# A conditioning matrix summed by GpSimd inside the first MLP, and twelve units of its kind ahead of the expert loop instead of sixteen

## Chip, core and metric

One core of a Trainium2 chip runs one program. The time is microseconds on the device for one execution. TensorE multiplies, VectorE, ScalarE and GpSimd work on tiles, SyncE (SP) issues DMAs.

## What is computed

Two blocks over 256 tokens of width 1024. The first has a mixer, cross-attention and a mixture of 32 experts (each 12.6 MB of float32 weights). The second has two layers, attention and then an MLP each, and every one of the four sublayers is conditioned on a vector `c`:

```python
def ada_modulation(c, w, b):
    m = jax.nn.silu(c) @ w + b
    shift, scale, gate = jnp.split(m[:, None, :], 3, axis=-1)
    return shift, scale, 1.0 + gate

def second_block(...):
    for layer in range(DEPTH_2):
        shift, scale, gate = ada_modulation(c, ada_w[layer, 0], ada_b[layer, 0])
        h = x * (1.0 + scale) + shift
        y = mixer_ab(...) if layer % 2 == 0 else mixer_c(...)
        x = layer_norm(DN_ALPHA * x + gate * y, ...)
        shift, scale, gate = ada_modulation(c, ada_w[layer, 1], ada_b[layer, 1])
        h = x * (1.0 + scale) + shift
        y = squared_relu_mlp(h, mlp_w1[layer], mlp_w2[layer])
        x = layer_norm(DN_ALPHA * x + gate * y, ...)
```

Each `ada_w` is 1024 x 3072, so that four of them are 50 MB, read for one vector-matrix product each.

## The kernel before

The weights come through SBUF slots of 2 MB, called granules; SP issues their DMAs in the order in which TensorE uses them, and waits for `granules_used` (`used`) before it overwrites a slot. An `ada_w` is cut into six units of 512 columns, 24 in all. A unit is 1024 x 512, 2 MB, and TensorE multiplies it against `cs`, which holds silu(c) in one column of 32 (`ada`, L1353). After a group of units ScalarE copies the bank out and `ada_combine` (L1365) adds up the quadrants. Units 0 to 15 stand ahead of the expert loop, at places given by `ADA_AT`, and fill TensorE's time there. Units 16 to 21 follow in the attention of the first layer (`late_main` L1779, `late_combine` L1789), units 22 and 23 in the attention of the second (`late3`), where VectorE copies their banks (`late_copies`, L2571).

Ahead of the loop the other weights are used in halves of 1 MB: ScalarE rounds a half (`half_hi`), VectorE takes the rest (`half_lo`), and TensorE multiplies three times (L1274). In order: `w_k`, `w_v`, `w_in`, `w_out`, `w_q`, `w_o`. `project(MEMT)` uses `w_v`. The expert loop streams 192 granules of 2 MB.

An MLP is 16 granules, w1 and w2 by turns, four to a turn of `mlp_group`: w1 (L1274 with `XT_r`) fills two banks, ScalarE takes ReLU (L1045) and square (L1048), VectorE the low part (L2701, L2705, which raises `mlp_lo`), and w2 (L1274 with `arena_r`) adds into four banks. Every granule is first split, by ScalarE into `w_hi` (L554) and VectorE into `w_lo` (L565). ScalarE's order is fixed: behind the two ReLUs of w1 granule g it splits granules g+2 and g+3, so granules 8 and 9 behind granule 6's. SP's loop (L726) issues fill n when TensorE is done with granule n-4. `gate_rows` (L1706) stands before the last group; the layer norm that follows the MLP needs it. GpSimd has nothing to do in the MLP.

Of the kernel before, what the change touches and what calls it, by code (L numbers as in the profile page):

```python
# [22 lines left out]
ALU = mybir.AluOpType  # L23
# [4 lines left out]
P = 128  # L28
# [72 lines left out]
LATE = 16  # L101
ADA_AT = [("k", 2), ("v", 3), ("mix", 4), ("q", 1), ("scores", 3), ("router", 3)]
ADA_GROUPS = [(0, 2, 7, 6), (2, 5, 7, 6), (5, 9, 3, 2), (9, 13, 6, 7), (13, 16, 1, 4)]
# [3 lines left out]
def pre_stream():  # L107
# [4 lines left out]
    for name, n in ADA_AT:  # L112
# [15 lines left out]
SIDE = {PRE.index(("ada", u)): SLOTS + i for i, u in enumerate((8, 9, 12, 13))}  # L128
SIDE_FILL = {8: 32, 9: 48, 12: 80, 13: 96}
# [5 lines left out]
HEAD = [("w_k", 0), ("w_k", 1), ("ada", 0), ("w_v", 0), ("ada", 1), ("w_v", 1), ("ada", 2), ("ada", 4), ("w_in", 0), ("ada", 3)]  # L135
TAIL = [("w_o", 0), ("w_o", 1), ("ada", 12), ("ada", 14), ("ada", 15), ("ada", 13)]
# [3 lines left out]
AHEAD = {("ada", 12): (0,), ("ada", 15): (1,), ("ada", 13): (2, 3, 4, 5)}  # L140
# [5 lines left out]
        + [("c_in", i) for i in range(6)] + [("late", 3)] + [("c_out", i) for i in range(2)] + [("mlp1", i) for i in range(16)])  # L146
R2 = 4
# [90 lines left out]
def build_program(nc, A, tab_d, dft_d, out_d):  # L238
    ctx = ExitStack()
    with ctx:  # L240
# [195 lines left out]
        def unit_parts(u):  # L436

            if u == 12:
                places = [XNf, arn(6144, 2048)]
            elif u in SIDE_FILL:  # L440
                places = [{8: slot(SLOTS - 1), 9: arn(2048, SLOT), 13: arn(0, SLOT)}[u]]
            else:
                places = [slot(slot_of(PRE.index(("ada", u))))]
# [70 lines left out]
        def half_hi(act, name, *hs):  # L514

            for h in hs:
                n = half_no(name, h)
                g, raw = half_raw(name, h)
                if n == 1:
                    act.wait_ge(sem("gain_landed"), 16)  # L520
                else:
                    act.wait_ge(landed[slot_of(g)], FILL[g])
# [61 lines left out]
        def _(sp):  # L584
# [3 lines left out]
            sp.dma_start(first[:, 0:2, :], src[:, 0:2, :]).then_inc(sem("gain_landed"), 16)  # L588
# [4 lines left out]
            def fill(g, name, i):  # L593
# [44 lines left out]
            for g in FILL_ORDER[2:]:  # L638
# [17 lines left out]
                if (name, i) == ("w_v", 1):  # L656
# [3 lines left out]
                                 A["norm_ffn"][0].rearrange("(j p k) -> p j k", p=P, k=2)).then_inc(sem("gain_landed"), 16)  # L660
# [41 lines left out]
            for name, i in POST:  # L702
                if name[:3] != "mlp":
                    if (name, i) not in POST[0:2]:
                        post_fill(name, i)
                    if (name, i) == ("ab_in", 2):
                        sp.wait_ge(sem("bias_lo"), 2)
                        sp.dma_start(nfin, A["norm_final"][None, :].to_broadcast((P, D))).then_inc(sem("nfin_landed"), 16)
# [7 lines left out]
                with sp.Fori(0, 4) as i:  # L716
                    for j in range(R2):
                        s = slot_of(g + j)
                        sp.wait_ge(used, i * R2 + (g + j - R2 + 1))
                        if j % 2 == 0:  # L720
                            src = w1[:, :, bass.ds(i * (2 * HW) + (j // 2) * HW, HW)]
                            dst = slot(s).rearrange("p (k n) -> p k n", k=8)
                        else:
                            src = w2[:, bass.ds(i * 8 + (j // 2) * 4, 4), :]
                            dst = slot(s).rearrange("p (k n) -> p k n", k=4)
                        sp.dma_start(dst, src).then_inc(landed[s], 16)  # L726
# [11 lines left out]
        def _(pool):  # L738
# [2145 lines left out]
```

## Time and profile before

| | |
|---|---|
| median of three runs | 1813.48 us (1813.35 to 1814.29) |
| the profiled execution, its own time | 1816.24 us |
| its span | 1814.3 us |
| TensorE busy | 96% |
| GpSimd busy | 1% |
| DMA, mean | 324 GB/s, 587.43 MB |
| TensorE's granted clock | 0.992 of full speed |

The span is what the rows below divide; the execution's own time has what lies around it. PE is TensorE, DVE VectorE, ACT ScalarE, POOL GpSimd, SP SyncE. A row of the timeline names the line of the kernel, the tiles written and read, shape and count, and in brackets the engine's idle time before it with what ended it. A float32 multiplication shows as two records.

### The profile page before, as it was taken

To read this page: it belongs to the slowest core of one execution; us is meant where nothing else is said; L and a number is where in the kernel's file an instruction comes from. 1 tells how busy PE (TensorE), PEld (TensorE's weight loads), DVE (VectorE), ACT (ScalarE), POOL (GpSimd) and SP (SyncE) were. 2 spreads that over 40 slices of the span, in tenths; PEclk is the share of its full clock that TensorE was granted. 3 is DMA by queue.
4 is the path that set the end of the run, shared out by engine and by line. 5 is a ranking of instruction groups with operands and counts; after the bars stand their busy time and mean duration, and the time that the engine had idled before them with its cause. 6 is when DMAs were issued, how large, how long until landed. Compare 5 with 4: busy or idle time off the path is not lost.

```text
span 1814.3 us, 24405 instructions
## 1 busy us (share of the span) xinstructions
PE 1743.7 (96%) x9906; PEld 1092.5 (60%) x9906; DVE 749.0 (41%) x1287; ACT 526.5 (29%) x698; POOL 26.6 (1%) x36
## 2 busy tenths in 40 slices
PE   8999999999999999999999999999899999999997
PEld 7688754444434434343434344375699888679986
DVE  4454342212212112121212121379865469676555
ACT  5344421111111111111111010248444453744442
POOL 0002000000000000000000000000000000000001
PEclk9999999999999999999999999998999999999999
DMA  9958899999999999999999999974355556435550
GB/s 350 348 212 336 316 404 426 428 427 428 428 428 428 428 428 428 429 429 428 428 429 428 429 429 429 418 282 177 116 186 185 192 194 228 153 116 185 185 208 24
DMA packets 96608, 587.43 MB, mean 324 GB/s; under 512 B 7150, under 2 KB 7364, under 8 KB 70948
## 3 DMA queue, kind: packets, MB, share of 16 engines
q1 hardware_dynamic: 95072, 582.27, 79.3%
q10 hardware_dynamic: 1476, 4.30, 0.7%
q8 instruction: 44, 0.72, 0.2%
q14 instruction: 16, 0.13, 0.0%
HBM read 585.51 MB, written 1.05 MB: 323 GB/s over the span
## 4 chain that ended last, share of the span: by engine, by line
PE 72%; DMA 20%; DVE 5%; ACT 2%; issue 1%; SPq 0%; DVEq 0%; ACTq 0%
PE bank L1274 31%; DMA ring<-in_w_gate_up 19%; PE bank L1587 15%; PE bank L1606 9%; PE bank L1533 4%; PE bank L1861 3%; PE bank L1353 1%; PE bank L1617 1%; PE bank L1265 1%; PE bank L1579 1%; DVE w_lo L565 1%; ACT arena L965 1%; DMA ring<-in_ada_w 1%; PE bank L1599 1%; PE bank L1988 0%
## 5 line engine op out<-in xcount | busy, mean ns | idle before, releaser
L1587 PE MATMUL bank<-ring,arena 128*64 128x512 f32 x2048 | 462.4, 597 | 28.4 <-DMA ring<-in_w_gate_up 27.8
L1587 PEld LDWEIGHTS bank<-ring,arena 128*64 128x64 f32 x2048 | 137.7, 136 | 319.3 <-issue 255.9
L1606 PE MATMUL bank<-ring,arena 128*64 128x512 f32 x1024 | 226.8, 595 | 3.3
L1274 PE MATMUL bank<-w_hi,arena_r 128*128 128x512 f32 x672 | 217.1, 391 | 1.9 <-DVE arena_r L2705 1.9
L565 DVE TENSOR_TENSOR w_lo<-ring,w_hi 128x4096 fp32r<-128x4096 f32 (+2 forms) x44 | 192.5, 4375 | 44.1 <-ACT w_hi L554 41.8
L2400 DVE TENSOR_SCALAR arena<-bank 128x512 f32<-128x512 f32 x32 | 22.1, 691 | 367.2 <-PE bank L1587 367.2
L963 ACT ACTIVATE arena<-arena,sb_tab 128x512 f32<-128x512 f32 x32 | 23.1, 722 | 508.7 <-DVE arena L2400 508.7
L554 ACT ACTIVATE w_hi<-ring 128x4096 fp32r<-128x4096 f32 (+2 forms) x43 | 152.3, 3583 | 31.6 <-DMA ring<-in_c_w_out 18.3
L1606 PEld LDWEIGHTS bank<-ring,arena 128*64 128x64 f32 x1024 | 71.9, 137 | 137.6 <-issue 132.1
L1274 PE MATMUL bank<-XT_r,w_hi 128*128 128x256 f32 x512 | 145.8, 285 | 4.4 <-DVE arena_r L2689 4.4
L1274 PE MATMUL bank<-arena_r,w_hi 128*128 128x256 f32 x512 | 144.9, 283 | 0.0
L1274 PE MATMUL bank<-XT_r,w_lo 128*128 128x256 f32 x512 | 144.9, 283 | 0.0
L1274 PEld LDWEIGHTS bank<-w_hi,arena_r 128*128 128x128 f32 x672 | 126.2, 188 | 29.3 <-DVE arena_r L2705 2.8
L1533 PEld LDWEIGHTS bank<-arena,sb_XN 128*128 128x128 f32 x1056 | 123.2, 192 | 26.9 <-issue 26.9
L1533 PE MATMUL bank<-arena,sb_XN 128*128 128x64 f32 x1056 | 128.4, 275 | 0.0
L1274 PE MATMUL bank<-w_lo,arena_r 128*128 128x512 f32 x304 | 118.6, 390 | 0.0
L2421 DVE SCALAR_TENSOR_TENSOR arena_r<-bank,sb_att,arena_r 128x512 fp32r<-128x512 f32 x32 | 24.0, 751 | 217.3 <-ACT arena_r L968 217.3
L1274 PEld LDWEIGHTS bank<-XT_r,w_hi 128*128 128x128 f32 x512 | 98.2, 192 | 5.8 <-issue 5.3
L1274 PEld LDWEIGHTS bank<-arena_r,w_hi 128*128 128x128 f32 x512 | 98.2, 192 | 0.9 <-issue 0.5
L1274 PEld LDWEIGHTS bank<-XT_r,w_lo 128*128 128x128 f32 x512 | 98.3, 192 | 0.0
L968 ACT ACTIVATE arena_r<-bank,sb_att 128x512 fp32r<-128x512 f32 x32 | 22.0, 687 | 231.0 <-PE bank L1606 231.0
L538 DVE TENSOR_TENSOR half_lo<-ring,half_hi 128x2048 fp32r<-128x2048 f32 x26 | 59.5, 2290 | 64.0 <-ACT half_hi L528 64.0
(415 smaller groups left out, 2104.6 us busy)
## 6 DMA issues: line engine op xcount, KB each, us to landing
ring<-in_w_gate_up SPq DMA_DIRECT2D x128, 2048.0 KB, 32.0
ring<-in_w_down SPq DMA_DIRECT2D x64, 2048.0 KB, 35.3
ring<-in_mlp_w SPq DMA_DIRECT2D x32, 2048.0 KB, 8.3
ring<-in_ada_w SPq DMA_DIRECT2D x21, 2048.0 KB, 13.1
ring<-in_c_w_in SPq DMA_DIRECT2D x6, 2048.0 KB, 7.7
ring<-in_w_in SPq DMA_DIRECT2D x4, 2048.0 KB, 8.8
ring<-in_w_v SPq DMA_DIRECT2D x2, 2048.0 KB, 9.6
ring<-in_w_out SPq DMA_DIRECT2D x2, 2048.0 KB, 11.9
```

Source lines behind the costliest of these rows:

```text
L538: eng.tensor_tensor(lo[:], half_raw(name, h)[1], hi[:].bitcast(F32), ALU.subtract).then_inc(sem("w_lo"), 1)
L554: ins = eng.activation(dst, raw, ACT.Copy) if on_act else eng.tensor_copy(dst, raw)
L565: eng.tensor_tensor(lo[:, 0:w], slot(slot_of(granule_no(name, i)), w), hi[:, 0:w].bitcast(F32), ALU.subtract).then_inc(sem("w_lo"), 1)
L963: act.activation(sig, gcl, ACT.Sigmoid, bias=zero, scale=1.702).then_inc(sem("e_sig"), 1)
L968: act.activation(y_hi, B[2][:], ACT.Copy, scale=slot_gate).then_inc(sem("e_y"), 1)
L1274: mm = pe.matmul(out, st[a], mv[b], start=start and a + b == 0, stop=stop and a == 1, skip_group_check=True)
L1533: mm = pe.matmul(B[3][:, k * CAP:(k + 1) * CAP], XN[:, t, k * P:(k + 1) * P], sel_tok[:, t, :], start=(t == 0), stop=(t == 1))
L1587: mm = pe.matmul(B[m][CAP * h:CAP * h + CAP, :], xe[:, 2 * j + kl, :], w[:, kl, m * D + h * HW:m * D + (h + 1) * HW], start=False, stop=(j ...
L1606: mm = pe.matmul(B[2][CAP * h:CAP * h + CAP, :], hT[:, c, CAP * j:CAP * j + CAP], w[:, c, h * HW:(h + 1) * HW], start=(j == 0 and c == 0), ...
L1861: mm = pe.matmul(b, x[:, k, t * P:(t + 1) * P], parts[wa][:, kl, width * c:width * c + width], start=k + xa + wa == 0, stop=False, skip_gr ...
L2400: dve.tensor_scalar(gcl, B[0][:], 7.0, None, ALU.min).then_inc(sem("e_clamp"), 1)
L2421: dve.scalar_tensor_tensor(y_lo, B[2][:], slot_gate, y_hi.bitcast(F32), ALU.mult, ALU.subtract).then_inc(sem("e_ylo"), 1)
```

## The change

`LATE` goes from 16 to 12: units 0 to 11 stand ahead of the loop, units 12 to 17 take the places that 16 to 21 had, and the last six, the whole matrix of the second MLP, go to the first MLP. There a unit comes in eight pieces of 128 x 512 (256 KB) through three places in the arena (`unit_raw`). GpSimd multiplies a piece by the column of silu(c) that belongs to it and adds it to the unit's sum (`unit_acc`, two places by turns); the first piece of a unit is a product alone, written to the sum. TensorE then sums over partitions by four multiplications with a column of ones (`unit_sums`), and one ScalarE copy reads all 24 columns. `late3`, its copies and combinations are gone. The SP and TensorE loops of the first MLP are written out, and its `gate_rows` stands behind the last w1 granule.

```diff
-LATE = 16
-ADA_AT = [("k", 2), ("v", 3), ("mix", 4), ("q", 1), ("scores", 3), ("router", 3)]
+LATE = 12
+ADA_AT = [("k", 0), ("v", 2), ("mix", 3), ("q", 1), ("scores", 3), ("router", 3)]
...
+        unit_raw = [arn(a, HW) for a in (4096, 4608, 7312)]
+
+        def unit_acc(n):
+
+            return XN[:, 1, HW * (n % 2):HW * (n % 2) + HW]
...
+                def unit_fill(m):
+
+                    w = A["ada_w_2"][1, 1].rearrange("(k p) n -> p k n", p=P)
+                    n = m // 8
+                    if m >= 3:
+                        sp.wait_ge(sem("unit_used"), 2 * (m - 2))
+                    else:
+                        sp.wait_ge(*upto("mlp0", "mlp_lo", 1))
+                    sp.dma_start(unit_raw[m % 3], w[:, m % 8, HW * n:HW * n + HW]).then_inc(
+                        sem(f"unit{m % 3}_landed"), 16)
+
+                if l == 0:
+                    for n in range(16):
+                        if n >= R2:
+                            for m in range(4):
+                                unit_fill(4 * (n - R2) + m)
+                        mlp_fill(n // 4, n % 4)
...
+            pool.wait_ge(*upto("mlp0", "mlp_lo", 1))
+            for m in range(48):
+                n, kl = m // 8, m % 8
+                pool.wait_ge(sem(f"unit{m % 3}_landed"), 16 * (m // 3 + 1))
+                raw, acc, by = unit_raw[m % 3], unit_acc(n), sil[:, 1, kl:kl + 1]
+                if kl == 0:
+                    if n >= 2:
+                        pool.wait_ge(sem("late_comb"), 6 + n - 1)
+                    pool.tensor_scalar(acc, raw, by, None, ALU.mult).then_inc(sem("unit_used"), 2)
+                else:
+                    pool.tensor_scalar(raw, raw, by, None, ALU.mult).then_inc(sem("unit_used"), 1)
+                    pool.wait_ge(sem("unit_used"), 2 * m + 1)
+                    pool.tensor_tensor(acc, acc, raw, ALU.add).then_inc(sem("unit_used"), 1)
...
+                    if l == 0 and last and p == 0:
+                        act.wait_ge(sem("late_comb"), 12)
+                        act.activation(mod[:, 3, :], B[6][:, 0:24], ACT.Copy).then_inc(sem("late_read"), 1)
+                    elif l == 0 and last:
+                        gate_rows(1)
...
-            project(MEMT, 0, between={2: first_units, 4: ada_combine, 6: mix_turn})
+            project(MEMT, 0, between={6: mix_turn})
             chunk_ready("mix", KC - 1)
-            ada(3)
+            pe.wait_ge(sem("cs"), 2)
+            ada(2)
...
-            ada(4)
+            ada(3)
...
+                    if l == 0 and p == 1:
+                        if last:
+                            pe.wait_ge(sem("late_read"), 3)
+                            gate_rows(1)
+                        elif it:
+                            unit_sums(it - 1)
...
+                    if l == 0 and last:
+                        unit_sums(2)
+
+            def unit_sums(i):
+
+                for n in (2 * i, 2 * i + 1):
+                    pe.wait_ge(sem("unit_used"), 16 * n + 16)
+                    for c in range(4):
+                        mm = pe.matmul(B[6][:, 4 * n + c:4 * n + c + 1], unit_acc(n)[:, c * P:(c + 1) * P], ones[:, 0:1],
+                                       start=True, stop=True)
+                    mm.then_inc(sem("late_comb"), 1)
```

SP's queue from the last fills before the first MLP on, before (the loop of four fills, whose ISA rows hold the wait) and then now:

```order
L684 DMA ring<-in_ab_w_out 128x4x1024 [waits granules_used] x2
L716 UNCONDITIONAL_BRANCH
L716 ISA
L726 ISA [waits granules_used]
L726 DMA ring<-in_mlp_w_2 128x8x512
L719 REGISTER_ALU
L726 ISA [waits granules_used]
L726 DMA ring<-in_mlp_w_2 128x4x1024
```

```order
L689 DMA ring<-in_ab_w_out 128x4x1024 [waits granules_used] x2
L732 DMA ring<-in_mlp_w_2 128x8x512 [waits granules_used]
L732 DMA ring<-in_mlp_w_2 128x4x1024 [waits granules_used]
L732 DMA ring<-in_mlp_w_2 128x8x512 [waits granules_used]
L732 DMA ring<-in_mlp_w_2 128x4x1024 [waits granules_used]
L742 DMA arena<-in_ada_w 128x512 [waits mlp_lo] x3
L742 DMA arena<-in_ada_w 128x512 [waits unit_used]
L732 DMA ring<-in_mlp_w_2 128x8x512 [waits granules_used]
L742 DMA arena<-in_ada_w 128x512 [waits unit_used] x4
L732 DMA ring<-in_mlp_w_2 128x4x1024 [waits granules_used]
```

Four pieces of `ada_w` now stand between two fills of `mlp_w`, in front of the later one; they wait for GpSimd (`unit_used`).

TensorE behind the w1 part of granule 6, before and then now (`w_hi_49` and `w_lo_50` are granule 7, w2):

```order
L1274 MATMUL bank<-arena_r,w_hi_55 128x256
L1274 MATMUL bank<-XT_r,w_lo_56 128x256
L1915 REGISTER_ALU
L1930 REGISTER_ALU [waits w_lo]
L1274 MATMUL bank<-w_hi_49,arena_r 128x512 [waits mlp_lo]
L1274 MATMUL bank<-w_lo_50,arena_r 128x512
```

```order
L1322 MATMUL bank<-arena_r,w_hi_55 128x256
L1322 MATMUL bank<-XT_r,w_lo_56 128x256
L1988 MATMUL bank<-sb_tab,sb_XN 128x1 [waits unit_used]
L1988 MATMUL bank<-sb_tab,sb_XN 128x1 x3
L1988 MATMUL bank<-sb_tab,sb_XN 128x1 [waits unit_used]
L1988 MATMUL bank<-sb_tab,sb_XN 128x1 x3
L1322 MATMUL bank<-w_hi_49,arena_r 128x512 [waits mlp_lo,w_lo]
L1322 MATMUL bank<-w_lo_50,arena_r 128x512
```

The sums of units 0 and 1 (L1988) have come in between the two granules. The same rows stand again behind granules 10 and 13.

GpSimd from the end of unit 1 to the first pieces of unit 2, which are all new:

```order
L828 TENSOR_SCALAR arena<-arena,sb_sil 128x512 [waits unit2_landed]
L830 TENSOR_TENSOR sb_XN<-sb_XN,arena 128x512 [waits unit_used]
L828 TENSOR_SCALAR arena<-arena,sb_sil 128x512 [waits unit0_landed]
L830 TENSOR_TENSOR sb_XN<-sb_XN,arena 128x512 [waits unit_used]
L826 TENSOR_SCALAR sb_XN<-arena,sb_sil 128x512 [waits late_comb,unit1_landed]
L828 TENSOR_SCALAR arena<-arena,sb_sil 128x512 [waits unit2_landed]
L830 TENSOR_TENSOR sb_XN<-sb_XN,arena 128x512 [waits unit_used]
```

The first product of unit 2 (L826) waits for `late_comb`, which TensorE's sums raise.

## Rows read from the trace of the kernel before

**Rows 1.** Page of the profile: its first line
```profile
span 1814.3 us, 24405 instructions
```

**Rows 2.** Busy time of each engine by stage (columns as in the first line)
```profile
core 0: us, PE busy (x) PEld busy (x) DVE busy (x) ACT busy (x) POOL busy (x), PEclk, DMA share, GB/s
76.00:78.90 2.90, 2.90 (x17) 0.49 (x9) 1.01 (x1) 0.00 (x0) 0.00 (x0) 0.60 0.97 395
272.00:590.00 318.00, 316.87 (x1669) 138.00 (x1670) 69.29 (x154) 38.74 (x47) 0.00 (x0) 1.00 1.01 428
...
1308.00:1492.00 184.00, 182.63 (x1165) 165.88 (x1166) 108.17 (x83) 83.43 (x57) 0.00 (x0) 1.00 0.50 177
```

**Rows 3.** Chain of waits, two waits for DMA: start us, us, what
```profile
60.55 12.97 DMA ring<-in_ada_w
593.19 33.56 DMA ring<-in_w_gate_up
```

**Rows 4.** TensorE in order, 46 to 140 us: start us, us, instruction
```profile
46.41 3.64 PE L1353 MATMUL bank<-ring,sb_cs 128*32 128x512 f32 x32
...
69.27 1.92 PE L1353 MATMUL bank<-ring,sb_cs 128*32 128x512 f32 x16
73.57 5.34 PE L1353 MATMUL bank<-ring,sb_cs 128*32 128x512 f32 x32 [2.38 <-DMA ring<-in_ada_w]
...
132.72 7.08 PE L1353 MATMUL bank<-ring,sb_cs 128*32 128x512 f32 x64
```

**Rows 5.** VectorE, two instructions of the head
```profile
44.95 2.29 DVE L538 TENSOR_TENSOR half_lo<-ring,half_hi 128x2048 fp32r<-128x2048 f32 x1 [5.36 <-ACT half_hi L528]
...
138.82 1.65 DVE L2289 SCALAR_TENSOR_TENSOR arena_r<-bank,sb_col,arena_r 128x256 fp32r<-128x256 f32 x4
```

**Rows 6.** First MLP around granule 8: DMA issue, ScalarE, VectorE, TensorE
```profile
1365.01 0.37 SPq L726 DMA_DIRECT2D ring<-in_mlp_w  x1
...
1388.65 7.13 ACT L554 ACTIVATE w_hi<-ring 128x4096 fp32r<-128x4096 f32 x2
...
1392.30 8.96 DVE L565 TENSOR_TENSOR w_lo<-ring,w_hi 128x4096 fp32r<-128x4096 f32 x2 [2.76 <-ACT w_hi L554]
...
1387.10 0.40 PE L1274 MATMUL bank<-w_hi,arena_r 128*128 128x512 f32 x1
...
1398.00 0.28 PE L1274 MATMUL bank<-XT_r,w_hi 128*128 128x256 f32 x1
...
1409.52 0.40 PE L1274 MATMUL bank<-w_hi,arena_r 128*128 128x512 f32 x1
```

**Rows 7.** DMAs by line: KB of one, median us from issue to landing
```profile
ring<-in_mlp_w SPq DMA_DIRECT2D x32, 2048.0 KB, 8.3
sb_X<-in_x SPq DMA_DIRECT2D x1, 1024.0 KB, 17.3
```

**Rows 8.** GpSimd's groups: count | busy us, mean ns of one
```profile
L538 POOL TENSOR_TENSOR half_lo<-ring,half_hi 128x2048 fp32r<-128x2048 f32 x2 | 9.2, 4614 | 91.6 <-ACT half_hi L528 91.6
L773 POOL CAST w_hi<-ring 128x1224 fp32r<-128x1224 f32 x3 | 3.5, 1206 | 910.0 <-DMA ring<-in_ab_w_in 910.0
```

**Rows 9.** End of the program: GpSimd beside VectorE
```profile
1800.11 0.69 DVE L2621 SCALAR_TENSOR_TENSOR sb_X<-sb_X,sb_XN 128x512 f32<-128x512 f32 x1
1803.97 2.36 POOL L790 TENSOR_TENSOR sb_X<-sb_X,arena 128x1024 f32<-128x1024 f32 x1 [214.15 <-ACT sb_X L1009]
1805.55 1.33 DVE L2621 SCALAR_TENSOR_TENSOR sb_X<-sb_X,sb_XN 128x512 f32<-128x512 f32 x1
```

**Rows 10.** Second attention: VectorE's four copies, TensorE's combination
```profile
1567.17 0.42 DVE L2571 COPY sb_vec<-bank 128x256 f32<-128x256 f32 x1
1567.84 0.74 DVE L2571 COPY sb_XN<-bank 128x256 f32<-128x256 f32 x2
...
1584.03 1.95 PE bank L1789 x16
```

**Rows 11.** First MLP, the second part of its last granule: TensorE
```profile
1481.00 0.50 PE L1274 MATMUL bank<-w_hi,arena_r 128*128 128x512 f32 x1 [0.95 <-DVE arena_r L2705]
```

More of the change, by code:

```diff
@@ L127 @@
 R1 = 8
-SIDE = {PRE.index(("ada", u)): SLOTS + i for i, u in enumerate((8, 9, 12, 13))}
-SIDE_FILL = {8: 32, 9: 48, 12: 80, 13: 96}
+SIDE = {PRE.index(("ada", u)): SLOTS + i for i, u in enumerate((4, 5, 8, 9))}
+SIDE_FILL = {4: 32, 5: 48, 8: 80, 9: 96}
 RING = [g for g in range(NPRE) if g not in SIDE]
@@ L134 @@
 E_BLOCK = 4
-HEAD = [("w_k", 0), ("w_k", 1), ("ada", 0), ("w_v", 0), ("ada", 1), ("w_v", 1), ("ada", 2), ("ada", 4), ("w_in", 0), ("ada", 3)]
-TAIL = [("w_o", 0), ("w_o", 1), ("ada", 12), ("ada", 14), ("ada", 15), ("ada", 13)]
+HEAD = [("w_k", 0), ("w_k", 1)]
+TAIL = [("w_o", 0), ("w_o", 1), ("ada", 8), ("ada", 10), ("ada", 11), ("ada", 9)]
 FILL_ORDER = ([PRE.index(p) for p in HEAD] + [g for g in range(NPRE) if PRE[g] not in HEAD + TAIL]
@@ L145 @@
         + [("ab_out", i) for i in range(2)] + [("mlp0", i) for i in range(16)]
-        + [("c_in", i) for i in range(6)] + [("late", 3)] + [("c_out", i) for i in range(2)] + [("mlp1", i) for i in range(16)])
+        + [("c_in", i) for i in range(6)] + [("c_out", i) for i in range(2)] + [("mlp1", i) for i in range(16)])
 R2 = 4
@@ L715, in _, with mlp_fill @@
                 w2 = A["mlp_w2_2"][l].rearrange("(k p) n -> p k n", p=P)
[L716 to L726, printed above, removed]
+                def mlp_fill(i, j):
+                    s = slot_of(g + j)
+                    sp.wait_ge(used, i * R2 + (g + j - R2 + 1))
+                    if j % 2 == 0:
+                        src = w1[:, :, bass.ds(i * (2 * HW) + (j // 2) * HW, HW)]
+                        dst = slot(s).rearrange("p (k n) -> p k n", k=8)
+                    else:
+                        src = w2[:, bass.ds(i * 8 + (j // 2) * 4, 4), :]
+                        dst = slot(s).rearrange("p (k n) -> p k n", k=4)
+                    sp.dma_start(dst, src).then_inc(landed[s], 16)
+                def unit_fill(m):
[13 more added lines that the diff above has]
+                        mlp_fill(n // 4, n % 4)
+                else:
+                    with sp.Fori(0, 4) as i:
+                        for j in range(R2):
+                            mlp_fill(i, j)
                 g += 16
@@ L774, in _, with with_norm @@
                     *((sem("w_hi"), 1) if kl == 2 else (sem("ab_in_hi"), 1)))
-            last = mod[:, 3, :]
+            m2, m3 = mod[:, 2, :], mod[:, 3, :]
+            def with_norm(m, l, n):
+                pool.wait_ge(sem("late_mod"), n)
+                pool.tensor_tensor(part[:, 2], m[:, 8:16], cols("ln_b_2", 3)[:, l], ALU.mult).then_inc(sem("late_mod"), 1)
+                pool.wait_ge(sem("late_mod"), n + 1)
+                pool.tensor_tensor(m[:, 0:8], m[:, 0:8], part[:, 2], ALU.add).then_inc(sem("late_mod"), 1)
+                pool.tensor_tensor(m[:, 8:16], m[:, 8:16], cols("ln_g_2", 3)[:, l], ALU.mult).then_inc(sem("late_mod"), 1)
@@ L785, in _ @@
+            pool.wait_ge(sem("late_read"), 3)
+            pool.tensor_tensor(m3, m3, ada_bT[:, 72:96], ALU.add).then_inc(sem("late_mod"), 1)
+            with_norm(m3, 2, 6)
             split_hi(pool, "c_out", 1, on_act=False)
-            pool.wait_ge(sem("late_read"), 3)
-            pool.tensor_tensor(last[:, 16:24], last[:, 16:24], ada_bT[:, 88:96], ALU.add).then_inc(sem("late_mod"), 1)
             pool.wait_ge(*upto("ln3", "ln_landed", 32))
@@ L951, in _ @@
             act.wait_ge(sem("bias_landed"), 16 * 8)
-            act.wait_ge(*done("ada", 13))
+            act.wait_ge(*done("ada", 9))
             for m in range(2):
@@ L1936, in mlp_group @@
                     mm.then_inc(used, 1)
-            def mlp(l):
-                with pe.Fori(0, 3) as it:
-                    mlp_group(l, it, False)
-                gate_rows(2 * l + 1)
-                mlp_group(l, 3, True)
+                    if l == 0 and last:
[7 more added lines that the diff above has]
+                    mm.then_inc(sem("late_comb"), 1)
+            def mlp(l):
+                if l == 0:
+                    for it in range(4):
+                        mlp_group(0, it, it == 3)
+                else:
+                    with pe.Fori(0, 3) as it:
+                        mlp_group(l, it, False)
+                    gate_rows(2 * l + 1)
+                    mlp_group(l, 3, True)
                 at[0] += 16
@@ L2561, in front @@
                                       ALU.subtract).then_inc(sem("nm"), 1)
-            def late_copies():
-                for u, b in ((LATE + 6, 6), (LATE + 7, 7)):
-                    if u == LATE + 6:
-                        dve.wait_ge(sem("late_mm"), 4)
-                    else:
-                        dve.wait_ge(*done("late", 3))
-                    for i, part in enumerate(late_part(u)):
-                        dve.tensor_copy(part, B[b][:, i * S:(i + 1) * S]).then_inc(sem("late_part"), 1)
             def attend(st, mask, ot, after_front):
```

107 lines of the change are left out of this document (41 added, 66 removed).

## Prediction

> **What bounds the kernel now.** The page first: TensorE is busy nearly throughout, so I read which wait ends last in each stage [rows 1, 2]. From 272 to 590 us the DMA engines carry 428 GB/s [rows 2], and from 593 us the chain of waits names `in_w_gate_up` once per two experts [rows 3]. A loop whose DMA never rests ends when the bytes have passed, so it moves by exactly as much as its start moves. Before the loop TensorE goes without gaps apart from a wait of 2.38 us for `in_ada_w` [rows 4]. In the first MLP TensorE is busy 182.63 of 184 us, with DMA at half load (177 GB/s) [rows 2]. There, what TensorE receives late, the program gets late.
>
> **The head: four units fewer.** One unit is 16 records of `ada`: 3.64 us for two units, 7.08 for four [rows 4], so 1.78 each.
> - Units 0 and 1 go from the middle of `project(MEMT)`: 3.6. But they covered VectorE: `half_lo` runs 44.95 to 47.24 [rows 5], and TensorE now wants that half at 46.41 [rows 4]. 0.8 comes back. Gain 2.8.
> - One combination (L1365, eight records) goes: half of the 1.95 of 16 such records [rows 10], less some overlap: 0.8.
> - `ada(3)` becomes `ada(2)`. Before, the first unit begins at 69.27; then comes a wait of 2.38 us for the second, which stood behind `w_in` in the queue (12.97 us) [rows 3]; and the two that follow take 5.34 where 46.41 shows 3.64 for the same [rows 4], since the granted clock fell to 0.60 behind the wait [rows 2], toward the 1.2 GHz level. The end is 78.91, 9.6 after the start. Now the units are asked for before all of `w_in`, so 3.6. Gain 6.0.
> - `ada(4)` becomes `ada(3)`: 1.8, but the output projection's second token tile waits for L2289, which ends at 140.47 [rows 5]; it would be wanted at 139.3. Gain 0.6.
>
> Sum 2.8 + 0.8 + 6.0 + 0.6 = **10.2 us**. All later issues into the ring follow TensorE or the splits behind it, so I let the experts' stream, and the loop's end, move by the same. Bounds: 8 if another cover is gone, 12 if nothing comes back. The work between loop and MLP has as many units as before: 0.
>
> **The first MLP, the queue.** Granules are numbered 0 to 15, even w1, odd w2; w1 takes 11.5 us on TensorE (1398.00 to 1409.52), w2 10.9 [rows 6]. SP asked for granule 8 at 1365.01, when granule 4 was done; ScalarE splits it from 1388.65, 3.57 us, VectorE from 1392.30, 4.48, and TensorE takes it at 1398.00 [rows 6]: slack 1.2 us behind ready data.
>
> Now four pieces stand before each fill from 4 on, and the fourth waits until the first of them is worked off. Piece 16 begins unit 2, whose sum goes where unit 0's is. It waits for `late_comb`, that is for TensorE's sums behind granule 6. So fill 8 can't be issued until granule 6 is done, the very time at which ScalarE wants it landed. The same holds for fill 12 and granule 10 (unit 4, piece 32). This is a mechanism of the written order and doesn't depend on how fast GpSimd is.
>
> Prices. A combination of two units, 16 records, is 1.95 us [rows 10]; a new sum is eight records: 0.9. A fill lands 8.3 us after its issue [rows 7], a piece (0.26 MB at 428 GB/s) adds 0.6. What is issued behind a large transfer lands behind it: `in_x` took 17.3 us for 1 MB [rows 7]. A GpSimd sum: 4614 ns for 2048 columns [rows 8], so 1.2 for 512. A product by one column a partition isn't in the trace: below, the cast of 1224 columns in 1206 ns, 0.5 [rows 8]; above, the sum's 1.2; I take 0.8, as it too reads one tile. A piece with its wait: 2.1.
>
> Step by step, in the time of before:
> - Granule 6 ends 1387.1, `late_comb` rises at 1388.2, product done 1389.3 (VectorE is at its own two), piece 19 and fill 8 issued by 1389.7, landed +8.9 = 1398.6. Split: +3.57 + 4.48 = 1406.7. Granule 8 starts 8.7 late, 1.8 of it the two sums.
> - Fill 9 waits for piece 20, landed behind fill 8 at 1399.2, done 1401.3; issued 1401.7, landed 1410.6, split 1418.7, and VectorE then still makes the hidden tile's low part (1.5: two instructions of 0.69, as one of that shape in [rows 9], and a wait): granule 9 at 1420.2, 10.7 late.
> - Fill 10 waits for a product alone: in time. Fill 11 issued 1424.4, landed 1433.3, in time but for sums (1.8): granule 11 at 1444.4, ended 1455.3.
> - `late_comb` 1443.7, fill 12 issued 1445.0, landed 1453.9, split 1462.0: granule 12 starts there, and granule 13 at 1475.5 by the steps of 9.
> - Granule 13 ends 1486.4, sums to 1488.2, granule 14 to 1499.7. Fill 15 is issued 1479.7, landed 1488.6; `c_in` 0 behind it 1493.5; ScalarE is at its split to 1497.1 before it takes up granule 14's ReLU, VectorE to 1501.6, then twice 1.5. The second part of granule 15 starts at 1504.5, not 1481.00 [rows 11]: **23.5 us later**.
>
> The moved gate rows cost the same in either place. Unrolled loops I cost at nothing: the head is straight code, and TensorE runs it without gaps.
>
> **What rides on it.** A two-input VectorE instruction took 1.33 us beside a GpSimd sum, 0.69 without it [rows 9]. On the path such pairs meet some two times: +1.3 (0 to 8). Behind its 2.38 us wait TensorE lost 5.34 - 3.64 = 1.7 us to the clock [rows 2, 4]; behind the two waits of 7 us I add that twice: +3.4 (0 to 8, for five waits).
>
> The Trainium skill (SBUF — State Buffer, "SBUF: two separate sides") says that a VectorE instruction with two SBUF inputs and a GpSimd instruction exclude one another for their whole length. The trace agrees: 1805.55 plus 1.33 ends 0.55 after GpSimd's sum does. What it would make of this MLP is the second rival.
>
> **The second attention.** VectorE's four copies (1567.17 to 1568.58) and TensorE's combination (1.95) stood on the chain [rows 10]. I take 1.2 of the first and 1.0 of the second, as the next weights are ready only then. Gain **2.2** (0 to 3.2).
>
> **Sum.** -10.2 + 23.5 + 1.3 + 3.4 - 2.2 = +15.8. The profiled span 1814.3 [rows 1] becomes 1830.1; its execution took 1816.24, 2.76 above the median of the three runs, so that I add the sum to the median: 1813.48 becomes **1829.3**.
>
> **Rivals.**
> - The forecast, 0.67: 1817 to 1837. Its lower end has both bounds of the last part at nothing, the head at 12 and a stall less.
> - The two engines' exclusion becomes a bound, 0.14. Per granule VectorE's two-input work is 4.48 [rows 6] and 1.4 us, GpSimd's four pieces 4 x (0.8 + 1.2) = 8.0, together 13.9 of the 11.2 that a granule takes. Behind each hard stall the fills then follow every 13.9 instead of 11.4 us, some 4 us more each: 1837.3. For it: [rows 9]; against it: TensorE's own stalls give the engines time. By the rule that the skill's page states, it would be this.
> - It comes out faster, 0.11: fill 8 isn't held. If piece 16 were done by 1380 (8.9 before ScalarE's 1388.65), the MLP would cost its six sums, 5.4, and the total be 1813.5 - 10.2 - 2.2 + 5.4 = 1806.5. Against it: the wait as written; for it, that I may have misread which sum frees unit 2's place.
> - More gain ahead of the loop, 0.05: 8.4 MB less at 428 GB/s are 19.6 us, if DMA and not TensorE set the experts' start: 1819.9. Against it: the fills there wait for TensorE's releases.
> - The loop takes the head's gain back, 0.03: 1839.5.
>
> A difference under 0.2% (3.6 us) is what a measurement here can't tell from none. Slower than 1817.1: 0.83; faster than 1809.9: 0.11; between: 0.06, from the lower edge of the forecast. Range 1815 to 1840: it holds the forecast and three rivals, and leaves out the faster case.
>
> **What would show it.** `w_in` starts near 69.3 on TensorE instead of 78.9, and the last expert ends 10 earlier. In the MLP TensorE waits some 7 us ahead of granules 8 and 12 for VectorE's `w_lo`, ScalarE waits for the DMA `in_mlp_w`, GpSimd waits long at the first product of units 2 and 4, and SP issues fill 8 only behind granule 6. Fills at their old distance would prove me wrong; so would a product far above 1.2 us, or a loop that ends where it did.

## The result, and the profile after

The changed kernel takes **1859.55 us** (median of six runs, 1856.74 to 1862.97) against 1813.55 us: ratio 1.0253, interval 1.0242 to 1.0264. Slower was forecast, but by 15.8 us; it is 46, outside the range. The profiled execution has a span of 1861.1 us, 46.8 above [rows 1].

Where the 46.8 are, from the chain of waits, here of the kernel before, then of the changed one (start, us, what):

```profile
1308.24 6.84 PE bank L1274 x55
1490.82 0.45 PE bank L1841 x4
1622.21 134.77 PE bank L1274 x864
```

```profile
68.46 3.06 PE bank L1322 x24
...
1299.67 33.87 PE bank L1322 x238
...
1538.20 0.45 PE bank L1878 x4
...
1667.32 136.18 PE bank L1322 x864
```

The first MLP begins 8.6 us earlier (1308.24 to 1299.67), lasts 238.5 instead of 182.6, **56.0 us more**; the second attention behind it is 2.3 shorter (131.4 to 129.1), and the same 864 records of the second MLP take 1.4 longer, as the clock of its first 53 us is 0.97. The forecast had 28.2 more for this MLP (23.5 + 1.3 + 3.4), so 27.8 of the 31 us that it missed are here. Busy time in it, before and after (columns as in [rows 2]):

```profile
1308.24:1490.82 182.58, 181.63 (x1158) 165.08 (x1159) 106.82 (x80) 82.55 (x55) 0.00 (x0) 1.00 0.50 178
```

```profile
1299.67:1538.20 238.53, 200.30 (x1206) 181.53 (x1207) 120.65 (x80) 83.65 (x56) 183.92 (x94) 0.91 0.53 190
```

TensorE is idle 38.2 us instead of 1.0, which gives 37.3 of the 56.0, and busy 18.7 longer. 4.8 of this are the six sums (0.8 each in the chain); the other 13.9 are the same records at a mean granted clock of 0.91 of full speed (2.4 GHz) instead of 1.00. What TensorE waits for (us in total, times, longest), and then GpSimd's groups:

```profile
PE bank L1322 <- DVE w_lo L570: 17.8, 3, 6.8
PE bank L1988 <- POOL sb_XN L830: 13.5, 1, 13.5
PE bank L1322 <- DVE arena_r L2746: 6.9, 4, 3.1
```

```profile
L828 POOL TENSOR_SCALAR arena<-arena,sb_sil 128x512 f32<-128x512 f32 x42 | 94.7, 2254 | 2.4 <-DMA arena<-in_ada_w 2.4
L830 POOL TENSOR_TENSOR sb_XN<-sb_XN,arena 128x512 f32<-128x512 f32 x42 | 64.9, 1545 | 3.5
L826 POOL TENSOR_SCALAR sb_XN<-arena,sb_sil 128x512 f32<-128x512 f32 x6 | 20.4, 3398 | 68.5 <-DMA arena<-in_ada_w 55.5 <-PE bank L1988 12.9
```

The three waits for `w_lo` end at 1403.9, 1435.8 and 1469.6: they are ahead of granules 8, 10 and 12. The first of them:

```profile
1403.92 0.39 PE L1322 MATMUL bank<-XT_r,w_hi 128*128 128x256 f32 x1 [4.86 <-DVE w_lo L570]
```

The prediction had 8 and 12. The wait of 13.5 us for the last sums, behind granule 13, it didn't have at all. GpSimd works without pause but for 12.9 us at the written hold and 2.4 for DMAs. The timeline around fill 10 shows why it has no time to spare (start, us, engine, line):

```profile
1396.49 1.57 POOL L828 TENSOR_SCALAR arena<-arena,sb_sil 128x512 f32<-128x512 f32 x1 [1.14 <-DMA arena<-in_ada_w]
1398.14 1.28 POOL L830 TENSOR_TENSOR sb_XN<-sb_XN,arena 128x512 f32<-128x512 f32 x1
1399.40 5.82 POOL L828 TENSOR_SCALAR arena<-arena,sb_sil 128x512 f32<-128x512 f32 x1
...
1412.40 6.25 POOL L826 TENSOR_SCALAR sb_XN<-arena,sb_sil 128x512 f32<-128x512 f32 x1
```

```profile
1399.44 4.43 DVE L570 TENSOR_TENSOR w_lo<-ring,w_hi 128x4096 fp32r<-128x4096 f32 x1 [11.60 <-ACT w_hi L559]
1411.38 5.33 DVE L570 TENSOR_TENSOR w_lo<-ring,w_hi 128x4096 fp32r<-128x4096 f32 x1 [7.51 <-ACT w_hi L559]
```

A product with nothing beside it is 1.56 to 1.57 us and a sum 1.28. The product that begins beside `w_lo` takes 5.82: 1.57 and nearly all of VectorE's 4.43. At 1411.38 it is the other way round first: `w_lo` takes 5.33, since a sum is still running, and then the product waits for it. SP's fills show what comes of it:

```profile
1313.68 0.43 SPq L732 DMA_DIRECT2D ring<-in_mlp_w  x1
...
1386.87 0.43 SPq L732 DMA_DIRECT2D ring<-in_mlp_w  x1
...
1399.82 0.43 SPq L732 DMA_DIRECT2D ring<-in_mlp_w  x1
...
1419.06 0.43 SPq L732 DMA_DIRECT2D ring<-in_mlp_w  x1
...
1497.11 0.43 SPq L732 DMA_DIRECT2D ring<-in_mlp_w  x1
```

Twelve fills, 4 to 15, from 1313.68 to 1497.11: one in 16.7 us, where TensorE uses a granule in 11.2. Four pieces of GpSimd's own time, 0.08 being the gap between product and sum, are 4 x (1.56 + 1.28 + 0.08) = 11.7; one `w_lo` that it can't run beside makes 16.1.

### The profile page after: what moved, and what is told of

It reads as the page before. It is cut to its first block, busy times and chain, and to the rows that moved or that the text cites. A ratio compares the mean times of both kernels' runs of the same rounds, so it can differ in the third digit from the quotient of the medians.

```text
span 1861.1 us, 24308 instructions
## 1 busy us (share of the span) xinstructions
PE 1747.9 (94%) x9834; PEld 1104.2 (59%) x9834; DVE 761.5 (41%) x1282; ACT 527.0 (28%) x697; POOL 210.0 (11%) x129
## 4 chain that ended last, share of the span: by engine, by line
PE 64%; DMA 22%; DVE 5%; POOL 4%; ACT 3%; issue 1%; SPq 0%; DVEq 0%; ACTq 0%; POOLq 0%
PE bank L1322 27%; DMA ring<-in_w_gate_up 20%; PE bank L1630 14%; PE bank L1649 8%; PE bank L1576 4%; PE bank L1898 2%; POOL arena L828 2%; PE bank L1660 1%; POOL sb_XN L830 1%; DMA arena<-in_ada_w 1%; DVE w_lo L570 1%; POOL sb_XN L826 1%; DMA ring<-in_mlp_w 1%; PE bank L1622 1%; PE bank L1313 1%
## 5 line engine op out<-in xcount | busy, mean ns | idle before, releaser
L570 DVE TENSOR_TENSOR w_lo<-ring,w_hi 128x4096 fp32r<-128x4096 f32 (+2 forms) x44 | 198.3, 4507 | 114.9 <-ACT w_hi L559 113.3
L1322 PE MATMUL bank<-XT_r,w_hi 128*128 128x256 f32 x512 | 150.6, 294 | 22.3 <-DVE w_lo L570 17.8
L1322 PE MATMUL bank<-arena_r,w_hi 128*128 128x256 f32 x512 | 149.2, 291 | 0.0
L1322 PE MATMUL bank<-XT_r,w_lo 128*128 128x256 f32 x512 | 149.2, 291 | 0.0
L1322 PEld LDWEIGHTS bank<-XT_r,w_hi 128*128 128x128 f32 x512 | 103.0, 201 | 24.6 <-DVE w_lo L570 19.1
L1322 PEld LDWEIGHTS bank<-arena_r,w_hi 128*128 128x128 f32 x512 | 102.9, 201 | 0.6 <-issue 0.2
L1322 PEld LDWEIGHTS bank<-XT_r,w_lo 128*128 128x128 f32 x512 | 102.6, 200 | 0.0
L828 POOL TENSOR_SCALAR arena<-arena,sb_sil 128x512 f32<-128x512 f32 x42 | 94.7, 2254 | 2.4 <-DMA arena<-in_ada_w 2.4
```

Of the source, the lines that this page charges most:

```text
L570: eng.tensor_tensor(lo[:, 0:w], slot(slot_of(granule_no(name, i)), w), hi[:, 0:w].bitcast(F32), ALU.subtract).then_inc(sem("w_lo"), 1)
L828: pool.tensor_scalar(raw, raw, by, None, ALU.mult).then_inc(sem("unit_used"), 1)
L1322: mm = pe.matmul(out, st[a], mv[b], start=start and a + b == 0, stop=stop and a == 1, skip_group_check=True)
```

## Experiments

The theories as the expectations name them: **A**, the forecast, is the written hold (piece 16 behind TensorE's sums after granule 6, piece 32 after granule 10). **B** is GpSimd's pace, its own time and VectorE's exclusive instructions; it is the forecast's second rival with a dearer product. **C** is the chain in SP's order (fill, piece landed behind it, work, next fill).

Times are medians; the kernel before took 1814.1 to 1814.7 beside them. The last column is the length of the first MLP in the profiled execution, from the start of ScalarE's first `XT_r` row ahead of it to that of the first behind it, which leaves out the head and the attention: it begins at 1305.5 before and somewhere between 1291.7 and 1298.0 in the kernels with the new head.

| kernel | us | ratio to before, interval | MLP |
|---|---|---|---|
| before | 1813.55 | | 185.8 |
| changed | 1859.55 | 1.0253 (1.0242, 1.0264) | 241.8 |
| 1 no pieces, sums stay | 1806.01 | 0.9958 (0.9944, 0.9972) | 189.9 |
| 2 small GpSimd work | 1824.23 | 1.0058 (1.0042, 1.0075) | 205.9 |
| 3 no hold | 1858.14 | 1.0240 (1.0223, 1.0257) | 239.8 |
| 4 no product | 1840.37 | 1.0145 (1.0128, 1.0162) | 221.7 |
| 5 small work, no hold | 1807.41 | 0.9960 (0.9947, 0.9972) | 190.0 |
| 6 GpSimd free | 1817.57 | 1.0018 (1.0007, 1.0028) | 192.3 |
| 7 GpSimd's own queue | 1890.12 | 1.0421 (1.0403, 1.0438) | 270.8 |
| 8 VectorE instead | 1808.20 | 0.9965 (0.9953, 0.9978) | 189.9 |
| 9 `w_lo` by a copy | 1837.55 | 1.0126 (1.0110, 1.0141) | 222.2 |
| 10 pieces behind the fill | 1862.94 | 1.0268 (1.0252, 1.0284) | 242.3 |
| 11 as 8, again | 1807.44 | 0.9961 (0.9948, 0.9975) | 190.0 |
| 12 copy, no hold | 1828.59 | 1.0076 (1.0059, 1.0093) | 211.2 |

**1. What is left without the pieces.**

```diff
-                        if n >= R2:
-                            for m in range(4):
-                                unit_fill(4 * (n - R2) + m)
...
-            for m in range(48):
-                n, kl = m // 8, m % 8
...
-                    pe.wait_ge(sem("unit_used"), 16 * n + 16)
```

> Leaves out the 48 pieces: their DMAs and GpSimd's products and sums; TensorE's 24 sums over partitions read what stands there, and stay where they are. It measures what is left of the change, the head, the second attention and the sums. From the profile of after the first MLP begins 8.6 us earlier than before, the second attention is 2.3 us shorter, the six sums are 6 x 0.8 = 4.8 us. Every theory: 1813.5 - 8.6 - 2.3 + 4.8 = 1807.4 us. A time well above it would say that the unrolled loops, the earlier start or the place of the gate rows cost something by themselves.

1806.0, 1.4 under the expected time, so no cost of the unrolled loops, of the place of the gate rows or of the earlier start is seen. The head and the attention gain, the sums cost 4.1 in the MLP, and all that makes the kernel slow is in the pieces: 1859.6 - 1806.0 = 53.6 us.

**2. Small work on GpSimd, everything else as it is.**

```diff
-                    pool.tensor_scalar(raw, raw, by, None, ALU.mult).then_inc(sem("unit_used"), 1)
+                    pool.tensor_scalar(raw[:, 0:8], raw[:, 0:8], by, None, ALU.mult).then_inc(sem("unit_used"), 1)
```

(and so the other two instructions)

> GpSimd's product and sum take 8 of the 512 columns of each piece (the rest of the sum is left out); all DMAs, waits and the order stay. Theory A (the forecast: the written hold, fill 8 behind granule 6 and fill 12 behind granule 10, is the main cost): both holds stay, some 7 us each and some clock: about 1825 us. Theory B (GpSimd sets the pace: four pieces of 1.56 + 1.28 us and a w_lo of 4.4 us that it can't run beside, 16 us a fill where TensorE needs 11.2): the pace is gone, what is left is the hold where it shows: 1808 to 1825. Theory C (the chain fill, piece behind it in the ring, work, next fill, 12.2 us a fill, is the cost): without GpSimd's time 10 us a fill, as under A.

1824.2, and TensorE's waits inside this MLP are the two that the prediction had, ahead of granules 8 and 12:

```profile
PE bank L1322 <- DVE w_lo L570: 12.2, 2, 6.6
```

The hold exists and costs what A says, but 35 us of the 53.6 went with GpSimd's time.

**3. No hold, all the work.**

```diff
-            return XN[:, 1, HW * (n % 2):HW * (n % 2) + HW]
+            if n < 2:
+                return XN[:, 1, HW * n:HW * n + HW]
+            return arn(5264 + HW * (n - 2), HW)
...
-                    if n >= 2:
-                        pool.wait_ge(sem("late_comb"), 6 + n - 1)
+                    if n == 2:
+                        pool.wait_ge(*upto("ln0", "ln_x", 2))
...
-            load_ln(1, upto("ln0", "ln_x", 2))
             mlp_group(0, 3, True, ("c_in", 0))
+            load_ln(1, (sem("late_comb"), 12))
```

> All the work stays; units 2 to 5 get sums of their own in the space of the layer norm's gains (whose load moves behind the last sum), so that no product waits for TensorE's sums. A: both holds gone, most of the 56 us that the MLP grew by goes, under 1835. B: GpSimd was busy or blocked for all but 12.9 (hold) and 2.4 (DMA) of its 196.6 us, so at most 12.9 come back: 1847 or more. C: as B.

1858.1: A fails as the explanation of the 46. GpSimd's busy time rose by most of what the hold had left idle. The rows are of the changed kernel and then of this one, from 1311 us to the end of GpSimd's work; POOL is the figure ahead of the clock:

```profile
1311.00:1510.00 199.00, 160.77 (x958) 144.89 (x956) 94.35 (x44) 68.56 (x40) 179.06 (x90) 0.91 0.58 206
```

```profile
1311.00:1512.00 201.00, 164.84 (x974) 148.06 (x973) 98.02 (x43) 67.22 (x40) 188.62 (x90) 0.90 0.56 196
```

179.1 against 188.6 for the same 90 instructions: the 12.9 us of idle time had hidden 9.5 us of `w_lo`, beside which it would have stood blocked, and waits for DMAs grew by 2.2. From first product to last sum it is 197.9 and 196.7. TensorE's waits stand elsewhere: 6.2 us for the last sums, 29.9 for the low part of the hidden tile (`arena_r`, the squared activations that w2 multiplies). ScalarE, in its fixed order, splits the next granules first, and waits up to 18.5 us for the DMA of one before it takes up the ReLU from which that tile is made.

**4. Without the product of 42 pieces, about half of GpSimd's work.**

```diff
-                    pool.tensor_scalar(raw, raw, by, None, ALU.mult).then_inc(sem("unit_used"), 1)
-                    pool.wait_ge(sem("unit_used"), 2 * m + 1)
-                    pool.tensor_tensor(acc, acc, raw, ALU.add).then_inc(sem("unit_used"), 1)
+                    pool.wait_ge(sem("unit_used"), 2 * m)
+                    pool.tensor_tensor(acc, acc, raw, ALU.add).then_inc(sem("unit_used"), 2)
```

> Leaves out the product of 42 pieces: GpSimd adds the raw piece to the sum; the first piece of each unit keeps its product, all waits stay. A: the hold stays, GpSimd's part in it is small: above 1845. B: GpSimd needs 4 x 1.35 + 4.4 = 9.8 us a fill, under TensorE's 11.2: the pace falls away and only the hold is left: about 1825. C: the chain is 12.2 - 1.6 = 10.6 us: also about 1825.

1840.4 fits neither: it is 15 above B's 1825 (and C's), and 5 below A's bound. 19 us went with the product, so GpSimd's time counts, but B's 9.8 us a fill, with `w_lo` in it, should have left the hold alone. TensorE still waits twice at the hold (14.0 us for `w_lo`, where kernel 2 has 12.2), and besides 5.1 for the hidden tile and 1.7 for the last sums. The sums now meet `w_lo` instead of the products, as their mean shows:

```profile
L829 POOL TENSOR_TENSOR sb_XN<-sb_XN,arena 128x512 f32<-128x512 f32 x42 | 92.2, 2195 | 25.2 <-DMA arena<-in_ada_w 18.9 <-POOL sb_XN L829 5.2 <-POOL sb_XN L826 1.0
```

2195 ns instead of 1280: 38 us of blocked time stay with half of the work. The blocking isn't a share of GpSimd's time; it comes about once for each `w_lo`. Why this kernel is 16 us above kernel 2 isn't worked out beyond these waits and the clock (0.93 against 0.97 from 1300 to 1510 us).

**5. Small work and no hold**, the edits of 2 and 3 together.

> Eight of 512 columns for GpSimd's instructions, as in the run before (the rest of each sum is left out), and no product waits for TensorE's sums. What stays is the order in SP's queue: four pieces ahead of each fill through three places. If the hold accounts for all of the 18 us between 1824.2 (small work, hold kept) and 1806.0 (sums alone): 1806 to 1809. If the chain fill, piece behind it, next fill is a cost of its own (theory C): 1812 or more.

1807.4, within noise of 1. So the hold is worth 16.8 us here (1824.2 - 1807.4), and the order in SP's queue, with three places, nothing by itself: C is no cost of its own.

**6. GpSimd works, and neither SP nor TensorE waits for it.**

```diff
-                raw, acc, by = unit_raw[m % 3], unit_acc(n), sil[:, 1, kl:kl + 1]
+                raw, acc, by = unit_raw[m % 2], unit_raw[2], sil[:, 1, kl:kl + 1]
```

(no DMAs for pieces, as in 1; in the second attention ScalarE waits for the end of GpSimd's work before it copies into the arena)

> GpSimd does 48 products and 42 sums of 512 columns without any DMA, on three tiles that stay where they are, and neither SP nor TensorE waits for it (the sums over partitions read what stands there; the sums of the last six units are left out). It measures what GpSimd's work costs by sitting beside VectorE alone. Theory B in its strong form (VectorE is slowed as much as GpSimd): each granule's w_lo starts up to 1.6 us late with 1.2 us of slack: 1810 to 1816. If only GpSimd pays: 1806 to 1808, with products of about 6 us in the trace wherever a w_lo runs.

1817.6, 11.6 above 1 and above both expected ranges. In the MLP it costs 2.4 us (192.3 to 189.9), with both engines paying:

```profile
L827 POOL TENSOR_SCALAR arena<-arena,sb_sil 128x512 f32<-128x512 f32 x42 | 107.5, 2560 | 4.1
L829 POOL TENSOR_TENSOR arena<-arena 128x512 f32<-128x512 f32 x42 | 87.5, 2083 | 3.5
```

```profile
L570 DVE TENSOR_TENSOR w_lo<-ring,w_hi 128x4096 fp32r<-128x4096 f32 x15 | 72.9, 4861 | 16.3 <-ACT w_hi L559 15.4
```

VectorE's `w_lo` is 4.86 us instead of 4.43. Another 6.8 arise because GpSimd isn't done with the MLP: it works until 1522.9, and the second attention, which it now overlaps, takes 131.5 us from `XT_r` to `XT_r` where kernel 1 has 124.7. ScalarE's added wait isn't the cause: when it comes to that copy, after 1537, GpSimd has long been done, and it waits for TensorE. From first product to last sum GpSimd needs 214.4 us: 48 pieces beside VectorE at its normal pace take more time than this MLP has, even when nothing holds them up.

**7. The pieces in GpSimd's own queue**, with the edit of 3.

```diff
+            def own_fill(m):
...
+                pool.dma_start(unit_raw[m % 3], w[:, m % 8, HW * n:HW * n + HW]).then_inc(sem(f"unit{m % 3}_landed"), 16)
```

> All the work; the pieces are issued by GpSimd on its own DMA queue, three ahead, and no product waits for TensorE, so that no fill of the MLP waits for a piece. B: the fills are on time, but 48 pieces at 16 us for four end about 190 us after 1303, at 1493, where TensorE wants the last sums at about 1458: 1806 + 35 = 1841. A: without hold and without the queue it is 1806 to 1812.

1890.1, 49 above what I expected. The fills are on time (no wait for `w_lo` is left), and TensorE waits 69.4 us for GpSimd's sums. What I had left out is the issue itself:

```profile
1404.65 1.28 POOL L840 TENSOR_TENSOR arena<-arena 128x512 f32<-128x512 f32 x1
1406.22 0.59 POOL L825 DMA_DIRECT2D arena<-in_ada_w  x1 [0.30 <-POOL arena L840]
1406.86 1.57 POOL L838 TENSOR_SCALAR arena<-arena,sb_sil 128x512 f32<-128x512 f32 x1
```

3.87 us a piece instead of 2.92, 43 us over the 45 issues inside the loop, on the engine that was already the bound.

**8 and 11. The same sums by VectorE**, at places where it waits anyway.

```diff
+UNIT_DO = {(0, "lo"): (0, 3), (1, 1): (3, 6), (1, "lo"): (6, 8), (2, 1): (8, 11), (2, "lo"): (11, 15)}
...
+                        dve.wait_ge(sem("unit_used"), m)
+                        dve.scalar_tensor_tensor(acc, raw, by, acc, ALU.mult, ALU.add).then_inc(sem("unit_used"), 1)
```

(five places for pieces, four for sums; each piece stands in SP's order where its place has come free, so that the hold is gone as well)

> All the work, by VectorE: one instruction of 0.69 us multiplies a piece and adds it to the sum, at places where VectorE waits anyway, five places for pieces, four for sums, and the pieces stand in SP's order where their places have come free. VectorE is busy 107 of 183 us in this MLP and gets 48 x 0.69 = 33 more. B: it is GpSimd that was too slow, so the head's gain stays: 1806 to 1809, faster than before by 5 us. A and C: the same, since no wait is left on the way of a fill. A time above 1812 would say that 256 KB pieces in the ring cost by themselves.

> The same kernel as in the run in which VectorE does the work (1808.2 us), with more rounds, for the interval: 1806 to 1810, ratio to before 0.996 to 0.998.

1808.2, and 1807.4 when repeated: 0.9961 of before, interval 0.9948 to 0.9975, all of the computation done. It is the fastest complete version here, 52 us under the changed kernel and 6.6 under the one before. One instruction takes a piece:

```profile
L2750 DVE SCALAR_TENSOR_TENSOR sb_XN<-arena,sb_sil,sb_XN 128x512 f32<-128x512 f32 x28 | 21.0, 749 | 2.0
```

0.75 us against GpSimd's 2.92, and the MLP is as long as in kernel 1 without any pieces.

**9. VectorE's instruction made shorter.**

```diff
+            if name == "mlp0":
+                eng.tensor_copy(lo[:, 0:w], raw).then_inc(sem("w_lo"), 1)
```

> As the changed kernel, but in the first MLP VectorE makes w_lo by a plain copy with one input (the rest after rounding is left out, so its value is too large); GpSimd's work is whole. If what blocks GpSimd for some 4.4 us a w_lo is an instruction with two inputs in SBUF (theory B in the form of the second rival), products of 6 us vanish beside w_lo, GpSimd needs 4 x 2.93 = 11.7 us a fill, and the hold and some chain are left: 1830 to 1840. If any large VectorE instruction slows GpSimd, it stays above 1850.

1837.6, inside the expected numbers, but not by the expected mechanism. The product beside the copy is blocked as well, only for a shorter time:

```profile
1387.78 1.26 POOL L833 TENSOR_TENSOR sb_XN<-sb_XN,arena 128x512 f32<-128x512 f32 x1
1389.02 3.69 POOL L831 TENSOR_SCALAR arena<-arena,sb_sil 128x512 f32<-128x512 f32 x1
```

```profile
1389.07 2.29 DVE L572 CAST w_lo<-ring 128x4096 fp32r<-128x4096 f32 x1 [13.11 <-ACT w_hi L559]
```

3.69 is 1.57 and most of the copy's 2.29. So it isn't the second input that excludes GpSimd here. The Trainium skill (SBUF — State Buffer, "SBUF: two separate sides") names a second case beside two inputs, VectorE's fast modes with two ports, and counts a float32 copy within SBUF among them. These rows agree: the copy, here into fp32r, takes 2.29 us for as many columns as the subtraction does in 4.43, and the product ends 1.35 us after it does. The test shortened the block by 2.1 us and VectorE's own time by as much, so it doesn't tell one from the other.

**10. The pieces behind the fill.**

```diff
-                        if n >= R2:
-                            for m in range(4):
-                                unit_fill(4 * (n - R2) + m)
                         mlp_fill(n // 4, n % 4)
+                        if n >= R2:
+                            for m in range(4):
+                                unit_fill(4 * (n - R2) + m)
```

> As the changed kernel, but SP issues each group of four pieces behind its fill instead of ahead of it. B: GpSimd's pace is the same, the fills come one group earlier, so the first stalls go and the sums at the end wait: the last piece still ends some 196 us after the first, 1850 to 1860, no real gain. C or A in the form that the order ahead of the fill is the cost: under 1840.

1862.9, 3 above the expected range. The waits for `w_lo` are gone, and three for GpSimd's sums stand in their place, in all of about the same size as TensorE's waits were:

```profile
PE bank L1988 <- POOL sb_XN L830: 40.9, 3, 22.8
```

This order doesn't mend the pace.

**12. Copy and no hold together**, the edits of 9 and 3.

> The last two edits together: w_lo in the first MLP by a one-input copy (the rest after rounding is left out) and no hold by TensorE's sums. With GpSimd's pace near TensorE's (11.7 us a fill against 11.2), the hold should now be worth what it was worth with small work (16.8 us between 1824.2 and 1807.4), where it was worth nothing beside the slow pace (1858.1 against 1859.6): 1837.6 - 16.8 = 1820.8, so 1816 to 1826. If the hold is worth nothing here either, 1835 or more, and the forecast's mechanism had no part at all.

1828.6, outside the expected 1816 to 1826: the hold is worth 9.0 us here, between the 16.8 beside small work and the 1.4 beside full work. The closer GpSimd comes to TensorE's pace, the more of the hold shows.

Kernels 3 and 12 have no hold and the same work on GpSimd; only `w_lo` differs. GpSimd's first product and last sum, in 3 and then in 12:

```profile
1312.42 1.57 POOL L828 TENSOR_SCALAR sb_XN<-arena,sb_sil 128x512 f32<-128x512 f32 x1 [55.72 <-DMA arena<-in_ada_w]
...
1507.84 1.26 POOL L832 TENSOR_TENSOR arena<-arena 128x512 f32<-128x512 f32 x1
```

```profile
1308.35 1.57 POOL L831 TENSOR_SCALAR sb_XN<-arena,sb_sil 128x512 f32<-128x512 f32 x1 [52.12 <-DMA arena<-in_ada_w]
...
1474.69 1.26 POOL L835 TENSOR_TENSOR arena<-arena 128x512 f32<-128x512 f32 x1
```

These are 196.7 and 167.6 us for twelve groups of four pieces, 16.4 and 14.0 a group. Own time and one instruction of VectorE give 11.7 + 4.4 = 16.1 and 11.7 + 2.3 = 14.0. So B's sum holds for both lengths of `w_lo`.

## Why the prediction was wrong

**Head, -10.2: right.** `w_in` starts at 68.46, forecast 69.3. The MLP begins 8.6 earlier in this execution, and 7.5 to 13.8 earlier in the ones with the same head, so that single executions are too coarse to test the last us or two.

**Second attention, -2.2: right**, 2.3.

**The queue, +23.5: the mechanism is there, but it isn't what bounds.** Take the price of the sums out (5.4) and 18 us are left for the hold; kernels 2 and 5 put it at 16.8, and in kernel 2 TensorE waits exactly ahead of two granules, 12.2 us in all. But with the full work on GpSimd, taking the hold away gives 1.4 us.

**The step that failed is "I take 0.8" for the product, and with it "A piece with its wait: 2.1".** The product takes 1.56, above my upper bound of 1.2, because I bounded it by a sum (two inputs) and leaned to a cast (one input). It reads one tile and still is dearer than the sum of two. A piece is 2.92 with its gaps. Four of them, 11.7 us, are by themselves over TensorE's 11.2. A product far above 1.2 us was among the signs that the prediction named for being wrong.

**The second failure is "On the path such pairs meet some two times: +1.3".** I priced the exclusion by the pairs of small instructions, at 0.64 us each. It should have been priced as what each `w_lo` of 4.43 us takes from an engine without slack: GpSimd's groups are 51 us longer than their own times (29, 11 and 11). The second rival had this mechanism. It added VectorE's and GpSimd's times to 13.9 us a granule, but let it act only behind the two hard stalls, and so came to 1837.3 instead of 1860; with 1.56 for the product its own sum, 4.48 + 1.4 + 4 x 2.84, is 17.2 a granule, and the fills came every 16.7. It had a chance of 0.14, and its argument against, that TensorE's stalls give the engines time, did not hold: the fills came every 16.7 us although TensorE stood for 38.

**Clock, +3.4: too small.** 13.9 us in this MLP. The forecast's was for two waits of 7 us, 14 in all, and 38 were waited: 0.36 us for each us waited instead of 0.24, so that more waiting explains most of it but not all. Behind the last waits the rows of the changed kernel show it: 0.63, toward the 1.2 GHz level, with 1.53 us of work in 15, then 0.89 in the 28 us after.

```profile
1496.00:1511.00 15.00, 1.53 (x9) 1.45 (x8) 6.68 (x2) 5.09 (x3) 13.36 (x7) 0.63 0.90 342
1511.00:1539.00 28.00, 28.00 (x159) 24.94 (x159) 17.62 (x20) 12.12 (x12) 4.86 (x4) 0.89 0.34 127
```

**What stays open.** In kernel 5 GpSimd is blocked by every `w_lo` too, and it costs nothing, as its own time is small; so the blocking costs only on top of the 11.7. What those 11.7 would cost without any blocking wasn't measured: every kernel that kept them also kept an excluding `w_lo`, a shorter one in kernels 9 and 12. So the 53.6 us aren't split between the two by a run. An estimate from kernels 1 and 12: twelve groups at 11.7 would take 140 us, 27 less than kernel 12's 167.6, while kernel 12's MLP is only 21 us longer than kernel 1's. By that, GpSimd's own time alone would have cost little, and the blocking on top of it nearly all; but the copy in kernel 12 shortens VectorE's own work too, so the estimate may give the blocking too much. Kernel 4's 15 us above B's number stay open as well.

## What to carry to other kernels

Before work goes to an engine that seems idle, add up its time per period of the loop against the period of the engine that must not wait, and put in every instruction of its neighbour that it can't run beside: 11.7 + 4.4 against 11.2 decided this case, and neither the other order in SP's queue nor GpSimd's own queue (kernels 10 and 7) changed it. A wait found in the written order may be real and yet worth nothing behind a slower pace, so look for the pace first. And where an operation isn't in the trace, keep the upper bound well above the nearest row.

## What the runs showed of the hardware

GpSimd's product of 512 columns by a column takes 1.56 us, its sum of two tiles 1.28; on 8 columns they take 0.30 and 0.20 when nothing stands beside them, and a product of 8 columns beside `w_lo` still takes 4.3:

```profile
1388.31 0.20 POOL L830 TENSOR_TENSOR sb_XN<-sb_XN,arena 128x8 f32<-128x8 f32 x1
1389.92 4.27 POOL L828 TENSOR_SCALAR arena<-arena,sb_sil 128x8 f32<-128x8 f32 x1 [1.41 <-DMA arena<-in_ada_w]
```

VectorE's copy of 4096 columns with one input, 2.3 us, blocks GpSimd as its subtraction of two tiles, 4.43 us, does: products beside them took 3.69 and 5.82 us. It goes the other way as well: a subtraction that came while GpSimd was at a sum took 5.33 us. GpSimd's time for a group of four pieces was its own time plus one such instruction: 16.4 and 14.0 us measured, 16.1 and 14.0 by the sum. And a DMA issued by GpSimd takes 0.59 us of its time, with 0.30 of waiting ahead of it.
